# Experts' rows of a mixture-of-experts layer: turned by VectorE from quarter rows instead of by TensorE

## The reference, cut to what matters

```
aff = softmax(xf @ w_router)
gate, idx = top_k(aff.T, cap)                 # cap = 128 of 1024 tokens, per expert and group
xe = xf[idx]
hid = silu(xe @ w_gate) * (xe @ w_up)         # per expert, 1024 x 1024 matrices
ye = (hid @ w_down) * gate
y = zeros.at[idx].add(ye)
```

## Time and profile before

| what | value |
|---|---|
| median of 3 runs | 2406.44 us (2403.4, 2406.44, 2409.67) |
| span of the profiled execution, first to last instruction | 2402.56 us; its own time is not listed apart from the three runs |
| granted TensorE clock, mean over the span | 0.989 |
| top-k stage | about 1240 to 1273 us |
| first matmul of expert 0 | 1285.3 us |
| last matmul | 2386.8 us |

### The profile page before, as it was taken

One profiled execution on the slowest core, in us unless ns is written; L12 is line 12 of the kernel. 1 busy time (PEld: TensorE's weight loads), 2 busy tenths in 40 slices (PEclk: granted clock), 3 DMA queues, 4 the chain that ended last, 5 costly groups with the idle time before them and its releaser, 6 DMA issues. The chain is left out here.

```text
span 2402.6 us, 35196 instructions
## 1 busy us (share of the span) xinstructions
PE 2296.1 (96%) x13583; PEld 1915.1 (80%) x13583; DVE 1208.7 (50%) x1881; ACT 1103.8 (46%) x1828; POOL 603.2 (25%) x676
## 2 busy tenths in 40 slices
PE   6999999999999999999947999999999999999997
PEld 4679989777899897667736888888888888888886
DVE  3222334554413346665566555544445556666655
ACT  4223444655433436665543444444444455555552
POOL 3004342443133324430021011111110122222434
PEclk9999999999999999999978999999999999999999
DMA  8835445658454459764547566666666678888785
GB/s 319 259 107 182 145 160 185 191 150 185 122 194 141 162 177 249 228 180 158 170 189 263 204 211 221 214 226 210 207 203 231 216 268 309 322 308 291 284 302 175
DMA packets 239040, 511.49 MB, mean 213 GB/s; under 512 B 36981, under 2 KB 128005, under 8 KB 235825
## 3 DMA queue, kind: packets, MB, share of 16 engines
q1 hardware_dynamic: 190960, 394.78, 49.0%
q0 software_dynamic: 47936, 114.77, 16.0%
HBM read 415.32 MB, written 93.69 MB: 212 GB/s over the span
## 5 line engine op out<-in xcount | busy, mean ns | idle before, releaser
L2492 DVE TENSOR_TENSOR moe_w_lo<-moe_wf,moe_w_hi 128x2048 fp32r<-128x2048 f32 x192 | 439.5, 2292 | 456.6 <-ACT moe_w_hi L2367 450.0
L2367 ACT ACTIVATE moe_w_hi<-moe_wf 128x2048 fp32r<-128x2048 f32 x192 | 367.8, 1916 | 551.4 <-PE moe_acc L2630 550.5
L2630 PE MATMUL moe_acc<-moe_w_hi,moe_x_hi 128*128 128x512 f32 x1024 | 401.7, 392 | 0.9 <-DVE moe_x_lo L2498 0.6
L2630 PE MATMUL moe_acc<-moe_w_hi,moe_x_lo 128*128 128x512 f32 x1024 | 398.9, 390 | 0.0
L2630 PE MATMUL moe_acc<-moe_w_lo,moe_x_hi 128*128 128x512 f32 x1024 | 398.4, 389 | 0.0
L2630 PEld LDWEIGHTS moe_acc<-moe_w_hi,moe_x_hi 128*128 128x128 f32 x1024 | 192.3, 188 | 40.7 <-DVE moe_x_lo L2498 0.8
L2630 PEld LDWEIGHTS moe_acc<-moe_w_hi,moe_x_lo 128*128 128x128 f32 x1024 | 192.2, 188 | 40.3
L2630 PEld LDWEIGHTS moe_acc<-moe_w_lo,moe_x_hi 128*128 128x128 f32 x1024 | 192.4, 188 | 38.9
L1793 PE MATMUL banks<-fr_w_hi,fr_h_hi 128*128 128x256 f32 x768 | 223.2, 291 | 0.0
L1793 PE MATMUL banks<-fr_w_lo,fr_h_hi 128*128 128x256 f32 x768 | 217.0, 283 | 0.0
L1793 PE MATMUL banks<-fr_w_hi,fr_h_lo 128*128 128x256 f32 x768 | 216.9, 282 | 0.0
(11 more groups left out here) (294 smaller groups left out, 4083.4 us busy)
## 6 DMA issues: line engine op xcount, KB each, us to landing
moe_wf<-in_w_expert_gate SPq DMA_DIRECT2D x64, 1024.0 KB, 4.9
moe_wf<-in_w_expert_up SPq DMA_DIRECT2D x64, 1024.0 KB, 4.9
moe_wf<-in_w_expert_down SPq DMA_DIRECT2D x64, 1024.0 KB, 5.8
fr_w_raw<-in_w_units SPq DMA_DIRECT2D x28, 1024.0 KB, 7.2
fr_bias<-in_na_bias SPq DMA_DIRECT2D x16, 1520.0 KB, 11.1
fr_a_w<-in_w_ada POOLq DMA_DIRECT2D x16, 1024.0 KB, 9.0
scratch_qk_t<-fr_stage SPq DMA_DIRECT2D x64, 256.0 KB, 2.5
scratch_vov<-fr_stage SPq DMA_DIRECT2D x96, 128.0 KB, 2.2
```

Of the source, the lines that this page charges most:

```text
L2367: nc.scalar.activation(w_hi[:, q, :, :], wf[:, q, :, :], ACT.Copy).then_inc(w_hi_ready, 1)
L2492: nc.vector.tensor_tensor(w_lo[:, q, :, :], wf[:, q, :, :], w_hi[:, q, :, :].bitcast(F32), ALU.subtract).then_inc(w_lo_ready, 1)
L2630: mm = nc.tensor.matmul(acc[:, j, b, :], x[:, g, k, :], w[:, q, a, h * HALF:(h + 1) * HALF], start=(k == 0 and i == 0), stop=(k == KC - 1 ...
```

## The change

From expert 1 on, the rows of an expert are gathered as quarter rows. `h2` is seen as 8192 rows of 256 features; for each group four indirect DMAs of 128 quarter rows are issued. The partition quarter `q` (32 partitions) receives feature quarter `q` of the 128 tokens, the tokens lying as 4 blocks `t` of 32 along the free dimension. VectorE then turns 32x32 blocks, one instruction for each group, into `x_raw`, which lies at the address of `x_lo`. ScalarE copies `x_hi` from `x_raw` and VectorE subtracts in place to get `x_lo`. TensorE's `turn_x` goes away. Since a partition `p` now holds features 8p to 8p + 7, the gate and up matrices are loaded so that partition `p` holds rows 8p to 8p + 7: a piece is a pair of adjacent rows (8 KB in one run) of each partition instead of two blocks of 128 rows. The down matrix is loaded as before. The indices for the quarter rows, four times the token's index plus the quarter, come from a copy of the indices (`index_rep`), four more transposes on TensorE and one VectorE instruction (`index_q`). Expert 0 is still gathered in whole rows and turned by TensorE, which now takes every eighth column.

```diff
+    by_rows = [io[f"w_expert_{n}"].rearrange("e (p q a) n -> e q p a n", p=P, a=PIECE) for n in ("gate", "up")]
+    mats = by_rows + [io["w_expert_down"].rearrange("e (q a p) n -> e q p a n", p=P, a=PIECE)]
+    h2_quarters = io["h2"].rearrange("t (q n) -> (t q) n", q=4)
...
+        with nc.sbuf_tensor("moe_x_raw", [P, 2, GROUPS, KC, P], F32) as x_raw:
+            pass
         x_lo = s.sb("x_lo", [P, 2, GROUPS, KC, P], F32R)
...
+            for q in range(4):
+                pool.drain()
+                nc.gpsimd.memset(quarter[q * QT:(q + 1) * QT, :], float(q))
+            pool.drain()
...
+            def gather(e, j):
+                if isinstance(e, int) and e == 1:
+                    pool.wait_ge(first_turned, ONE + BK)
+                    pool.wait_ge(quarters_ready, 1)
+                else:
+                    pool.wait_ge(x_turned, ONE + (e - 1) * GROUPS)
...
                 for g in range(GROUPS):
+                    for t in range(4):
+                        at = index_q[:, t, col(e, g)] if isinstance(e, int) else idx_in[:, j, t, g:g + 1]
+                        pool.indirect_dma_start(quarter_rows(g)[:, t, :], None, h2_quarters,
+                                                bass.IndirectOffsetOnAxis(ap=at, axis=0)).then_inc(gathered[g], 16)
...
                         if is_last(e) and half:
-                            pool.wait_ge(x_turned, ONE + (e + 1) * BK)
+                            pool.wait_ge(x_turned, ONE + e * GROUPS)
...
+            def x_out(e, j):
+                for g in range(GROUPS):
+                    act.wait_ge(x_turned, ONE + (e - 1) * GROUPS + g + 1)
+                    nc.scalar.activation(x_hi[:, j, g, :, :], x_raw[:, j, g, :, :], ACT.Copy).then_inc(x_hi_ready, 1)
...
                     split(e + 1, GATE, range(0, 2))
-                    turned_out(e + 1, (x_hi[:, 1 - j], 1 - j), x_turned, x_hi_ready)
+                    x_out(e + 1, 1 - j)
...
             nc.vector.scalar_tensor_tensor(index_f[:, :], early[:, :], row0[:, :], late_f[:, ::-1], ALU.add, ALU.add).then_inc(top_ready, 1)
+            dve.drain()
+            each_slot = index_f[:, :].rearrange("r (t n) -> r t n", t=4).unsqueeze(2).to_broadcast([R, 4, 4, QT])
+            nc.vector.tensor_copy(index_rep[:, :, :, :], each_slot).then_inc(rep_ready, 1)
...
+            dve.wait_ge(rep_turned, 1)
+            dve.wait_ge(ready, ONE + 1)
+            nc.vector.tensor_scalar(index_q[:, :, :].rearrange("p t r -> p (t r)"), acc[:, 1, 0, 0:4 * R], 4.0, quarter[:, :],
+                                    ALU.mult, ALU.add).then_inc(quarters_ready, 1)
...
+            def turn_x(e, j):
+                dve.wait_ge(piece_done, ONE + piece(e - 1, GATE, NP))
+                for g in range(GROUPS):
+                    dve.wait_ge(gathered[g], e * 64)
+                    columns = quarter_rows(g).rearrange("p t (c m) -> p t m c", m=KC)
+                    turned = x_raw[:, j, g, :, :].rearrange("p m (t r) -> p t m r", t=4)
+                    nc.vector.transpose(turned, columns).then_inc(x_turned, 1)
+
+            def x_out(e, j):
+                for g in range(GROUPS):
+                    dve.wait_ge(x_hi_ready, ONE + (e - 1) * GROUPS + g + 1)
+                    nc.vector.tensor_tensor(x_lo[:, j, g, :, :], x_raw[:, j, g, :, :], x_hi[:, j, g, :, :].bitcast(F32),
+                                            ALU.subtract).then_inc(x_ready, 1)
...
+                    turn_x(e + 1, 1 - j)
                     split(e + 1, GATE, range(0, 2))
-                    turned_out(e + 1, x_hi[:, 1 - j], x_lo[:, 1 - j], 1 - j, x_hi_ready, x_ready)
+                    x_out(e + 1, 1 - j)
...
+            pe.wait_ge(rep_ready, 1)
+            for t in range(4):
+                mm = nc.tensor.transpose(acc[:, 1, 0, t * R:(t + 1) * R], index_rep[:, t, :, :].rearrange("r q n -> r (q n)"), ident[0:R, 0:R])
+            mm.then_inc(rep_turned, 1)
...
+            def turn_first(g):
+                pe.wait_ge(first_x[g], 16)
+                columns = xe[:, g, :].rearrange("t (c m) -> t m c", m=KC)
...
-                    products(e, UP, j, x_hi[:, j], x_lo[:, j], range(1, 2))
-                    turn_x(e + 1, 1 - j)
-                    products(e, UP, j, x_hi[:, j], x_lo[:, j], second)
-                    pe.wait_ge(x_ready, ONE + e * BK + 2 * BK)
+                    products(e, UP, j, x_hi[:, j], x_lo[:, j], range(1, NP))
+                    pe.wait_ge(x_ready, ONE + (e + 1) * GROUPS)
+                    pe.wait_ge(ye_ready, ONE + e * GROUPS)
                     products(e + 1, GATE, 1 - j, x_hi[:, 1 - j], x_lo[:, 1 - j], first)
```

More of the change, by code:

```diff
@@ L2114, in experts @@
     mod_row = io["mod"].rearrange("g (m n) -> g m n", n=D)
-    mats = [io[f"w_expert_{n}"].rearrange("e (q a p) n -> e q p a n", p=P, a=PIECE) for n in ("gate", "up", "down")]
+    QT = P // 4
+    by_rows = [io[f"w_expert_{n}"].rearrange("e (p q a) n -> e q p a n", p=P, a=PIECE) for n in ("gate", "up")]
+    mats = by_rows + [io["w_expert_down"].rearrange("e (q a p) n -> e q p a n", p=P, a=PIECE)]
+    h2_quarters = io["h2"].rearrange("t (q n) -> (t q) n", q=4)
     with ExitStack() as ctx:
@@ L2132, in experts @@
         zero = s.sb("zero", [P, D])
-        idx_in = s.part([P, 2, GROUPS], U32)
+        index_rep = s.part([R, 4, 4, QT])
+        index_q = s.part([P, 4, R], U32)
+        quarter = s.part([P, 1])
+        idx_in = s.part([P, 2, 4, GROUPS], U32)
         idx_out = s.part([P, 2, GROUPS], U32)
@@ L2165, in experts @@
         gcol_ready = s.sem("gcol_ready")
-        gathered = s.soft_sem("gathered")
+        gathered = [s.soft_sem(f"gathered{g}") for g in range(GROUPS)]
+        first_turned, first_hi_ready, first_ready = (s.sem(f"first_{n}") for n in ("turned", "hi_ready", "ready"))
+        rep_ready, rep_turned, quarters_ready = (s.soft_sem(n) for n in ("rep_ready", "rep_turned", "quarters_ready"))
         x_turned = s.sem("x_turned")
@@ L2261, in _, with gather_first @@
             by_expert = lambda t, e: t[:, :].rearrange("p (g e) -> p g e", g=GROUPS)[:, :, bass.ds(e, 1)].squeeze(2)
-            def gather(e, j, first=False):
-                if not first:
-                    pool.wait_ge(x_turned, ONE + e * BK)
+            def gather_first():
+                for g in range(GROUPS):
+                    at = bass.IndirectOffsetOnAxis(ap=index_c[:, col(0, g)], axis=0)
+                    pool.indirect_dma_start(xe[:, g, :], None, io["h2"], at).then_inc(first_x[g], 16)
+                    if g == 0:
+                        nc.gpsimd.memset(row0[:, :], 0.0).then_inc(first_begun, 1)
+            def gather(e, j):
[4 more added lines that the diff above has]
+                    pool.wait_ge(x_turned, ONE + (e - 1) * GROUPS)
                 if not isinstance(e, int):
-                    nc.gpsimd.tensor_copy(idx_in[:, j, :], by_expert(index_c, e))
+                    by_quarter = index_q[:, :, :].rearrange("p t (g e) -> p t g e", g=GROUPS)
+                    nc.gpsimd.tensor_copy(idx_in[:, j, :, :], by_quarter[:, :, :, bass.ds(e, 1)].squeeze(3))
                     pool.drain()
                 for g in range(GROUPS):
[L2271 to L2274, removed]
+                    for t in range(4):
+                        at = index_q[:, t, col(e, g)] if isinstance(e, int) else idx_in[:, j, t, g:g + 1]
+                        pool.indirect_dma_start(quarter_rows(g)[:, t, :], None, h2_quarters,
+                                                bass.IndirectOffsetOnAxis(ap=at, axis=0)).then_inc(gathered[g], 16)
             def scatter(e, j):
@@ L2291, in scatter @@
                                             compute_op=ALU.add).then_inc(added, 16)
-            gather(0, 0, True)
+            gather_first()
             gather(1, 1)
@@ L2635, in products, with turn_h @@
                         mm.then_inc(half_done, 1)
-            def turn(rows, j, done, bs=range(BK)):
+            def turn_first(g):
+                pe.wait_ge(first_x[g], 16)
+                columns = xe[:, g, :].rearrange("t (c m) -> t m c", m=KC)
+                for b in range(2 * g, 2 * g + 2):
+                    for k in range(4):
+                        mm = nc.tensor.transpose(acc[:, 0, b, k * P:(k + 1) * P], columns[:, b % 2 * 4 + k, :], ident[:, :])
+                    mm.then_inc(first_turned, 1)
+            def turn_h(e, j, bs=range(BK)):
+                pe.wait_ge(hid_ready, ONE + e * BK + bs[-1] + 1)
                 for b in bs:
```

31 lines of the change are left out of this document (13 added, 18 removed).

## The result

The changed kernel takes 2409.67 us (median of 20 runs, 2404.5 to 2418.33) against 2403.77 us (median of 20, 2402.36 to 2409.67) of the kernel before: ratio 1.0028, 95% interval 1.002 to 1.0035. **The forecast of 2380.5 us was wrong; the 26 us did not come.** The profiled execution took 2404.5 us with a span of 2402.7. It is the fastest of the twenty, so the trace shows less of the loss than the median has.

The account below looks back on a forecast made before the run. TensorE, busy 96% of the span, was taken as the bound; -26.7 + 0.2 + 0.5 = -26.0 us gave a 2376.6 us span, and with 3.9 us around it 2380.5 us, range 2374 to 2390.

Parts of the forecast that it names:

- TensorE's turn: Rows' turn of experts 1 to 15 leaves TensorE: 15 x 1.78 us, -26.7 us in all.
- VectorE's turn: Two 128x1024 turns at each period's head, 1.3 to 2.5 us each, costing nothing below 5.1 us per instruction.
- The second rival: VectorE's turn over 5.1 us: TensorE idles before gate matmuls for x_lo; 12 us at 5.5 us each; chance 4%.
- x_hi and x_lo from SBUF: ScalarE's and VectorE's split of gathered rows: no more work than before, 4.2 us to spare, cost 0.
- Weights as pairs of rows: Gate and up loads in 8 KB runs: landing slightly faster to three times slower, no cost by itself.
- The start: Before expert 0's matmuls: +0.2 us for VectorE's index copies, +0.5 us for TensorE's strided transposes.
- the +1.8 us: Upper bound at the start, if expert 0's 16 transposes of columns 8 words apart take twice as long.
- Gathers as quarter rows: POOL issues eight indirect DMAs instead of two, delaying unit loads: cost 0, bounds 0 to 3 us in five experts.
- The eight take 10 to 17 us: POOL's time for eight gathers, from two earlier ones of 1.03 and 1.84 us with 0.3 us between.
- They start 7 to 9 us into the period: POOL's gathers wait on VectorE's turn, so may start earlier than the 12.6 us under TensorE's turn.
- TensorE bears 5.7 us: Spare before the down products: h_lo ready at 2038.5, products starting at 2044.3, so ScalarE's wait is hidden.
- The first rival: POOL late: gathers of 2.75 us each delay fy loads, TensorE stops 3.7 us in five experts; +18 us, chance 5%.

Follow-up runs that it names:

- experiment 1: Changed kernel, with POOL loading the first two units of results ahead of the eight gathers instead of behind them: 2374.29 us, ratio 0.9886.
- experiment 4: Kernel before, with gate and up weights as pairs of adjacent rows and TensorE turning every eighth column for all 16 experts: 2403.63 us, ratio 1.0002.
- Experiment 10: Kernel before with eight quarter-row gathers, TensorE's turn kept, eight matmuls left out in each of 15 experts (1.82 us shorter period): 2386.42 us, ratio 0.9931.

## Why the prediction was wrong

**TensorE's turn, -26.7 us: right.** The period shrank to 67.05 us, and with the queue mended 2374.3 and 2375.3 us come out, the latter by a change on two other engines.

**VectorE's turn, below 5.1 us free: right where the period isn't late,** and the size in the range of 1.3 to 2.5:

```profile
L2548 DVE STREAM_TRANSPOSE moe_x_raw<-moe_xe x30: 2110/2138/2178, 1310.9 to 2277.9; 128x1024 f32<-128x1024 f32 x30
```

2.14 us (minimum, median and maximum in ns), nearly twice the one-pass add of 1.23. The rule of the Trainium skill on 16-byte lines (SBUF — State Buffer, "Door 1: The DMA port swizzle") would have it slower too; but no run here turns solid rows on VectorE, so how much of the 2.14 us is the step's isn't shown. Behind expert 0 one wait of TensorE is for x_lo, 1.86 us at 2286.70: expert 14's period was late already, the turn began 12.8 us into it instead of 4.4, and then its 4.2 us were not covered. The second rival's sign was there once, though the turn is far below 5.1 us. The other rule of the Trainium skill, which sends a full transpose to TensorE (VectorE: DVE Perf Modes, "Rules for kernel authors"), would have been the worse choice here: the kernel before goes by it and takes 2403.8 us, experiment 1 does not and takes 2374.3.

**x_hi and x_lo from SBUF, cost 0: wrong in one respect.** They were on time but for that one wait, but x_lo now holds up POOL's gathers. That x_lo left PSUM for SBUF was seen as a matter of duration only.

**Weights as pairs of rows, 0: right** (experiment 4). **The start, +0.7 us: half of it.** From TensorE's dead transposes at 1271.0 to the first matmul of expert 0 at 1283.26 it is 12.3 us, before 11.95 (1273.37 to 1285.32), so the start costs 0.3. The strided turns hold TensorE hardly longer than solid ones: eight take 0.81 us where they took 0.79. The weight loads under them are slower, though, 193 ns against 140 (changed kernel, then the kernel before):

```profile
L2703 PEld LDWEIGHTS moe_acc<-moe_parts,moe_xe x16: 186/193/207, 1280.5 to 1289.5; 128*128 128x128 f32 x16
...
L2641 PEld LDWEIGHTS moe_acc<-moe_parts,moe_xe x256: 138/140/143, 1282.6 to 2285.0; 128*128 128x128 f32 x128
```

So these loads pay for the stride, which agrees with the same rule of the Trainium skill on 16-byte lines (SBUF — State Buffer, "Door 1: The DMA port swizzle"), but the transposes cover it; the +1.8 us that were allowed for did not come.

**Gathers as quarter rows, "Cost 0, bounds 0 to 3 us in each of five experts": the step that failed.** Four things in it, each in the trace:
- *The eight take 10 to 17 us.* They took 18.2 us in expert 9 and 16.2 to 21.9 later. The range was built of the two durations of the earlier trace rows without asking what made 1.84 of 1.03. In the kernel before, seven pairs of gathers between 1396 and 1815 us had taken 4.1 to 4.4 us a pair. The prediction cites the port rule and lets it change nothing; VectorE's own order of time stood beside it.
- *They start 7 to 9 us into the period.* True in expert 9 (8.9), not afterwards: 12.1 in expert 10 and up to 13.2. A late square makes the results late, these stand ahead of the next pieces and the turn on VectorE, the turn releases the gathers. One late period makes the next one later by 3 us. The step was priced for one period and multiplied.
- *TensorE bears 5.7 us.* That spare was read in a period of 68.85 us, with "two turns" before the down products where the changed kernel has one. The way POOL, load, squares, down piece, h_hi, h_lo isn't tied to TensorE's pace once it is late, while the down products come 1.78 us sooner. The removal of TensorE's turn ate a third of the spare that was to hide the rest of the change. In expert 9 h_lo ended at 1951.65 + 2.48 = 1954.13 and the products began at 1955.56: 1.4 us left. In expert 10 there was none.
- *Stops have a price of their own.* After the longest two, and one of 2.4 us, matmuls ran at 0.43 us a step before they came back to 0.227, 6 us in all.

The first rival was this mechanism, at the very place, and worked out at +18 us. It was given 5% since it was tied to gathers of 2.75 us each. It needed no such thing: 18 us for eight, in a shorter period, that carried their lateness over. Experiment 10 shows that even 14 us are too many there. And its price was half of what was lost, 33 us, since neither the carrying over nor the slow steps were in it.

Two small terms of the base were off as well, the same way. The three runs that the forecast started from have a median of 2406.44 us, twenty have 2403.77. And a profiled execution's time is 1.7 to 1.9 us above its span (2404.5 and 2402.7 in the changed kernel, likewise in every experiment), not 3.9.

## What to carry to other kernels

When a change shortens the period, take its gain off every spare that was read in the old one, before the spare is used to hide the rest of the change. Where work is added on a queue, look at what waits behind it for somebody else: an order in which urgent small loads go ahead of a large piece of work that nobody wants for 45 us costs one moved line, and so does an engine's own order in which nothing that the bottleneck needs stands behind a wait for DMA. Then follow a late period into the next one, since lateness that comes back to its own start adds up. And when one part is put back in an experiment, read where the others went with it: the long period also brought the gathers' end forward by 2.4 us.

## What was not expected of the hardware

- A gather of rows on POOL took 0.95 us with VectorE idle, in PSUM, or turning, and ended 0.8 to 0.9 us behind a VectorE operation with two SBUF operands that was running when it began: up to 3.1 us for one such, and four times in thirteen traces 7.29 to 9.49 us for four or five in a row without a gap. The plain unit loads kept their 0.53 to 0.63 us under the same operations.
- A 32x32-block turn of 128x1024 fp32 on VectorE read at a step of 32 bytes took 2.14 us, and TensorE's weight loads at the same step 193 ns instead of 140, which its transposes covered (0.81 us for eight, 0.79 in solid rows).
- The granted clock after a stop, in the changed kernel's order of time around its longest pause:

```profile
2232.17 0.39 PE L2691 MATMUL moe_acc<-moe_w_hi,moe_x_lo 128*128 128x512 f32 x1
2239.64 0.79 PE L2691 MATMUL moe_acc<-moe_w_hi,moe_h_hi 128*128 128x512 f32 x1 [7.08 <-DVE moe_h_lo L2539]
2240.23 0.63 PE L2691 MATMUL moe_acc<-moe_w_lo,moe_h_hi 128*128 128x512 f32 x1
```

  and two stretches by the view of busy times (columns as in the earlier trace rows):

```profile
2230.00:2245.00 15.00, 7.92 (x29) 6.09 (x28) 10.27 (x12) 10.97 (x15) 2.96 (x4) 0.77 0.29 104
...
2240.30:2242.80 2.50, 2.50 (x8) 1.91 (x7) 2.42 (x3) 2.05 (x5) 0.44 (x1) 0.50 0.42 174
```

  The granted clock of the whole stretch is 0.77, and 0.50 right behind the stop. There TensorE works at the lower level, 1.2 GHz, with steps of 0.43 us where 0.227 stood at 2.4 GHz; the stop was all that the engine did before the clock fell. A pause doesn't always do it: behind the one of 2.37 us at 2094.88 the steps went to 0.43 us too, behind those of 2.68 us at 2025.32 and 2.47 us at 2312.91 they stayed at 0.227.
